# First layer's modulation in two channel chunks on TensorE's column groups, with three projection units interleaved and x loaded first

## The reference

```python
cond_act = silu(cond)                        # c for latent, c_ctx for context tokens
for layer in range(2):
    shift, scale, gate = split(cond_act @ w_mod[layer] + b_mod[layer], 3)
    hm = rmsnorm(x, norm_g[layer]) * (1 + scale) + shift
    if layer == 0:                           # Fourier mixer A | gated conv mixer B
        u_a, z_a, b_b, c_b, v_b, z_b = split(hm @ w_in, 6)          # w_in: 1024 x 6144
        y_a = fft2(u_a in 4 groups of 256 channels, ortho).real * silu(z_a)
        y_b = b_b * dwconv3(c_b * v_b) * silu(z_b)
        out = concat(y_a, y_b) @ w_out
    else:
        out = bidirectional SSD mixer(hm)    # the longer part of the kernel
    x = x + gate * out
return rmsnorm(x, final_norm_g), states
```

## Time and profile before

| | us |
|---|---|
| median of 3 executions | 1209.58 |
| lowest, highest | 1209.22, 1210.56 |
| the profiled execution's own time | 1210.87 |
| its span, first to last instruction | 1208.9 |
| PE busy in it | 1136.6 |
| DVE busy, ACT busy, POOL busy | 792.9, 441.8, 280.5 |

### The profile page before, as it was taken

How to read it: one execution, slowest core, us unless ns; L and a number is a source line. 1 busy time by engine, 2 the same in 40 slices (tenths; PEclk the granted TensorE clock), 3 DMA queues, 4 the chain that set the end, 5 groups by cost and what they waited for, 6 DMA issues and landing times. The chain is left out here.

```text
span 1208.9 us, 19168 instructions
## 1 busy us (share of the span) xinstructions
PE 1136.6 (94%) x7179; PEld 1044.7 (86%) x7179; DVE 792.9 (66%) x1385; ACT 441.8 (37%) x846; POOL 280.5 (23%) x422
## 2 busy tenths in 40 slices
PE   6899999999999999999889999898989898978997
PEld 1389999999999998888889989898989898967786
DVE  1553444467666434547779797979797979786454
ACT  3331222122211133335544544454535453544321
POOL 1110000000000000012043534444443535463001
PEclk9899999999999999999999999999999999989999
DMA  8642223254544243214334333434342424272702
GB/s 332 188 148 68 84 85 104 56 183 128 158 135 143 88 176 102 83 35 158 85 95 123 101 110 105 126 105 127 99 121 87 125 80 144 71 265 63 295 30 87
DMA packets 175670, 148.04 MB, mean 122 GB/s; under 512 B 6844, under 2 KB 156708, under 8 KB 175220
## 3 DMA queue, kind: packets, MB, share of 16 engines
q1 hardware_dynamic: 170996, 130.29, 34.6%
q0 software_dynamic: 4608, 16.83, 4.1%
HBM read 134.31 MB, written 12.78 MB: 122 GB/s over the span
## 5 line engine op out<-in xcount | busy, mean ns | idle before, releaser
L261 DVE TENSOR_TENSOR w_lo<-raw_w,w_hi 128x1024 fp32r<-128x1024 f32 x128 | 157.0, 1230 | 94.6 <-ACT w_hi L255 93.0
L290 PE MATMUL PS<-h_hi,w_hi 128*128 128x320 f32 x768 | 177.2, 312 | 6.1 <-DVE h_lo L364 5.2
L290 PE MATMUL PS<-h_lo,w_hi 128*128 128x320 f32 x768 | 175.6, 310 | 0.0
L290 PE MATMUL PS<-h_hi,w_lo 128*128 128x320 f32 x768 | 175.5, 310 | 0.0
L255 ACT ACTIVATE w_hi<-raw_w 128x1024 fp32r<-128x1024 f32 x128 | 134.2, 1052 | 110.1 <-PE PS L290 72.2
L290 PEld LDWEIGHTS PS<-h_hi,w_hi 128*128 128x128 f32 x768 | 128.4, 189 | 11.2 <-issue 4.0
L290 PEld LDWEIGHTS PS<-h_hi,w_lo 128*128 128x128 f32 x768 | 129.0, 188 | 0.0
L290 PEld LDWEIGHTS PS<-h_lo,w_hi 128*128 128x128 f32 x768 | 128.9, 188 | 0.0
L1320 PE MATMUL PS<-h_hi,w_hi 128*128 128x320 f32 x480 | 118.9, 330 | 10.4 <-DVE big L1509 10.4
L1320 PE MATMUL PS<-h_lo,w_hi 128*128 128x320 f32 x480 | 111.7, 315 | 0.0
L1320 PE MATMUL PS<-h_hi,w_lo 128*128 128x320 f32 x480 | 111.6, 314 | 0.0
(11 more groups left out here) (223 smaller groups left out, 2257.7 us busy)
## 6 DMA issues: line engine op xcount, KB each, us to landing
raw_w<-in_fc_w_in_dram SPq DMA_DIRECT2D x48, 512.0 KB, 4.6
raw_w<-in_ssd_w_in_dram SPq DMA_DIRECT2D x48, 512.0 KB, 5.1
big<-l_scr SPq DMA_DIRECT2D x40, 512.0 KB, 4.1
big<-in_w_mod_dram POOLq DMA_DIRECT2D x16, 1024.0 KB, 5.4
raw_w<-in_fc_w_out_dram SPq DMA_DIRECT2D x16, 512.0 KB, 3.6
raw_w<-in_ssd_w_out_dram SPq DMA_DIRECT2D x16, 512.0 KB, 7.8
big<-in_w_mod_dram SPq DMA_DIRECT2D x6, 1024.0 KB, 18.0
y_scr<-big SPq DMA_DIRECT2D x40, 128.0 KB, 1.8
```

Source lines behind the costliest of these rows:

```text
L261: dve.tensor_tensor(w_lo[:, slot, :], raw_w[:, slot, :], w_hi[:, slot, :].bitcast(F32), ALU.subtract).then_inc(lo_ready, 1)
L290: mm = pe.matmul(PS[:, 2 * pair + s, 0:HALF], w[:, slot, ws], h[:, kt, s * HALF:(s + 1) * HALF], start=(kt == 0 and n == 0), stop=(kt == K ...
```

## The change

- SP loads x first, as five DMAs of one token tile each, then the parameters. The constants and the conditioning vectors are issued on ACT's queue.
- `w_mod`'s shift and scale columns are treated in two chunks: chunk c has channels 512c to 512c+511 of both. A chunk is eight DMAs, one for each set of 128 rows, of 512 KB (2 KB pieces). There is one buffer, so chunk 1 is issued when PE has used chunk 0; units 0 to 2 are loaded between them.
- `cond` is padded with zeros to 32 columns (`condp`). The eight row sets are multiplied in four column groups: row set 4·half+q goes to PSUM partitions 32q to 32q+31. The sum over the groups is made by the product that also turns the row into a column, with a (128, 2) constant `group_sum` as moving operand.
- Shift and scale of channel tiles 0 to 3 are finished from chunk 0, and their `h` made, before chunk 1.
- Units 0, 1 and 2 are summed side by side in three pairs of banks, each in two parts: channel tiles 0 to 3 and 4 to 7.
- ACT does the norm before the SiLU of `cond`.

```diff
-        wm = [carve(5120, 2, 1024), raw_w[:, 0:2, :], raw_w[:, 2:4, :], *(carve(5120 + 2048 * n, 2, 1024) for n in (1, 2, 3)),
-              carve(23808, 2, 1024), carve(5120, 2, 1024)]
+        wm = carve(5120, KT, 2, 512)
+        condp = carve(21504, KT, 32)
...
+        def mod_pe(pe, c):
+            for half in range(2):
+                pe.wait_ge(wm_landed[2 * c + half], 64)
+                for s in range(2):
+                    for q in range(4):
+                        t = 4 * half + q
+                        mm = pe.matmul(PS[32 * q:32 * q + 32, 6 + s, :], condp[:, t, :], wm[:, t, s, :],
+                                       start=(half == 0), stop=(half == 1))
+            mm.then_inc(wm_used, 1)
+        def mod_T_pe(pe, c):
+            pe.wait_ge(mod_copied, c + 1)
+            for j in range(8):
+                mm = pe.matmul(PS[:, 6, 2 * j:2 * j + 2], mod_sb[:, j // 4, (j % 4) * P:(j % 4 + 1) * P], group_sum,
+                               start=True, stop=True)
+            mm.then_inc(mod_T, 1)
...
         def start_pe(pe):
+            for t in range(3):
+                norm_pe_tile(pe, t)
             pe.wait_ge(par_landed, 16 * PAR_DMAS)
             pe.transpose(PS[:, 6, 0:P], praw[:, 0, :], ident)
...
+            for t in range(3, NT):
+                norm_pe_tile(pe, t)
+            pe.wait_ge(cond_padded, 1)
+            pe.wait_ge(par_ready, 2)
+            mod_pe(pe, 0)
+            mod_T_pe(pe, 0)
+            unit_part_pe(pe, 0, range(0, 4))
+            pe.wait_ge(ss_step, 1)
+            mod_pe(pe, 1)
+            unit_part_pe(pe, 1, range(0, 2))
+            mod_T_pe(pe, 1)
+            unit_part_pe(pe, 1, range(2, 4))
+            for u, kts in ((2, range(0, 4)), (0, range(4, 8)), (1, range(4, 8)), (2, range(4, 8))):
+                unit_part_pe(pe, u, kts)
...
+            chunk_load(0)
+            first_load(0)
+            first_load(1)
+            first_load(2)
+            sp.wait_ge(wm_used, 1)
+            chunk_load(1)
+            first_load(3)
+            sp.wait_ge(wm_used, 2)
             sp.dma_start(dft_g, A["dft_group"]).then_inc(dft_landed, 16)
...
+            norm_act(act)
             act.wait_ge(cond_landed, 32)
             act.activation(cond[:, :, :], cond[:, :, :], ACT.Silu).then_inc(cond_ready, 1)
-            norm_act(act, 0, xn, xT0)
-            for u in range(2):
-                split_hi(act, u, u)
-            act.wait_ge(wm_used, 8)
-            act.activation(mod_sb[0:2, 0:1024], PSf[0:2, 0:1024], ACT.Copy).then_inc(mod_copied, 1)
...
+            split_hi(act, 0, 0)
+            mod_copy_act(act, 0)
+            split_hi(act, 1, 1)
+            for k in range(4):
+                h_act(act, k)
+            split_hi(act, 2, 2)
+            mod_copy_act(act, 1)
+            for k in range(4, KT):
+                h_act(act, k)
+            split_hi(act, 3, 3)
...
+            split_lo(dve, 0, 0)
+            dve.wait_ge(par_ready, 2)
+            ss_dve(dve, 0)
+            split_lo(dve, 1, 1)
+            h_dve(dve, 0)
+            split_lo(dve, 2, 2)
+            ss_dve(dve, 1)
+            h_dve(dve, 1)
+            split_lo(dve, 3, 3)
```

More of the change, by code:

```diff
@@ L361, in h_dve @@
+        def h_dve(dve, c):
+            dve.wait_ge(ss_ready, c + 1)
+            if c == 0:
+                dve.wait_ge(xt_done, NT)
+            for k in range(4 * c, 4 * c + 4):
+                for seg, (a, b) in enumerate(SEGS):
+                    dve.tensor_scalar(xT0[:, k, a:b], xT0[:, k, a:b], ss_mod[:, 1, seg, k:k + 1], ss_mod[:, 0, seg, k:k + 1],
                                       ALU.mult, ALU.add).then_inc(v_done, 1)
                 if k % 2:
-                    dve.wait_ge(hh_done, KT * layer + k)
@@ L373, in h_act @@
[L373 to L376 removed]
+                pool.wait_ge(hh_done, k + 1)
+                pool.tensor_tensor(h_lo[:, k, :], xT0[:, k, :], h_hi[:, k, :].bitcast(F32), ALU.subtract).then_inc(h_odd_ready, 1)
+        def h_act(act, k):
+            act.wait_ge(v_done, 2 * (k + 1))
+            act.activation(h_hi[:, k, :], xT0[:, k, :], ACT.Copy).then_inc(hh_done, 1)
@@ L708, in build_step, with mod_copy_act, unit_part_pe @@
         eh_done, el_done = sem("eh_done"), sem("el_done")
+        def mod_pe(pe, c):
+            for half in range(2):
+                pe.wait_ge(wm_landed[2 * c + half], 64)
+                for s in range(2):
+                    for q in range(4):
[9 more added lines that the diff above has]
+            mm.then_inc(mod_T, 1)
+        def mod_copy_act(act, c):
+            act.wait_ge(wm_used, c + 1)
+            act.activation(mod_sb, PS[:, 6:8, :], ACT.Copy).then_inc(mod_copied, 1)
+        def unit_part_pe(pe, u, kts):
+            if kts[0] == 0:
+                pe.wait_ge(lo_ready, u + 1)
+            for kt in kts:
+                if u == 0:
+                    h_wait(pe, 0, kt)
+                ws = slice(kt * P, (kt + 1) * P)
+                for n, (w, h) in enumerate(((w_hi, h_hi), (w_hi, h_lo), (w_lo, h_hi))):
+                    for s in range(2):
+                        mm = pe.matmul(PS[:, 2 * u + s, 0:HALF], w[:, u, ws], h[:, kt, s * HALF:(s + 1) * HALF],
+                                       start=(kt == 0 and n == 0), stop=(kt == KT - 1 and n == 2))
+            if kts[-1] == KT - 1:
+                mm.then_inc(unit_used, 1)
         def start_pe(pe):
+            pe.wait_ge(cst_landed, 16)
+            for t in range(3):
+                norm_pe_tile(pe, t)
             pe.wait_ge(par_landed, 16 * PAR_DMAS)
@@ L768, in fourier_act @@
                 act.wait_ge(unit_used, 4 * i + k + 1)
-                src = pair_view(k % 2)
+                src = pair_view(2 if first and k == 2 else k % 2)
                 if k < 2:
@@ L1855, in _ @@
             dve.memset(ones[:, :], 1.0).then_inc(ones_ready, 1)
+            for t in range(4):
+                norm_dve_tile(dve, 0, xn, t)
             dve.wait_ge(par_T, 1)
@@ L1905, in _ @@
             norm_pool(pool, 0)
-            h_pool(pool, 0, xT0)
+            h_pool(pool)
             mod_pool(pool)
```

174 lines of the change are left out of this document (59 added, 115 removed).

## The result

| | before | after |
|---|---|---|
| median of 4 executions each, us | 1209.4 | 1193.6 |
| lowest, highest | 1209.09, 1210.56 | 1192.75, 1194.93 |
| profiled execution, its span | 1210.87, 1208.9 | 1192.75, 1190.7 |
| first DFT product starts | 85.35 | 69.19 |

The ratio after to before is 0.9869, 95% interval [0.9852, 0.9886]: 15.8 us faster. I had expected 1193.6 within 1 us and a first block of the modulation of 5.3 to 6.1 us; that block took 5.01, so both were missed on the fast side.

What follows compares the result with a forecast made beforehand. The kernel was taken as a PE stream whose start alone could shrink: first DFT product from 85.35 to 70.7, 14.6 us earlier, so 1210.87 becomes 1196.3, less 1.3 for the median gives 1195.0 us; range 1190 to 1202.

Steps and rivals of the forecast that it cites:

- What bounds the kernel: Whole kernel: a PE stream; the first DFT product's start shifts 14.6 us, and the end with it.
- Loads: Start: x lands by 10.2 us, chunk 0 by 21.4, three units' weights by 26.7; chunk 1 by 40.8.
- Norm: ACT's chain and token transposes at 2.2 us each: last copy ends at 19.9, modulation may start at 21.8.
- Column groups: Modulation: a set costs 1.03 us, a chunk 4.1 instead of 13.8; slow start 1.9; chunk 0 used up at 27.8.
- h of 0 to 3, half unit: After chunk 0: h starts at 31.9, tile 3 enters PE 7.6 us later at 39.5, PE free at 40.4.
- From chunk 1 to the DFT: From 44.6: 28 channel tiles take 24.6 us, group sum 1.1, small waits 0.4; DFT starts at 70.7.
- Later loads: Later modulation weights, issued at 57.5, margin 9 us; rival that late slices give the gain back: 1209, chance 0.04.
- slower pieces: Rival on chunk loads: 2 KB pieces at 294 GB/s, 14.3 us a chunk; 1197.8, or 1201.6 with a bubble; chance 0.12.
- latencies paid one by one: Rival on chunk loads: eight loads don't overlap, 28.8 us a chunk, DFT at 104, 1228 us; chance 0.01.
- groups that don't overlap: Rival on modulation: each matmul costs 0.86 us, a chunk 13.8; DFT at 90.0, 1214.2 us; chance 0.05.
- Quicker start: Rival on the start: full PE clock early, modulation at 20.8, chunk 0 done at 25.0; 17.5 us earlier, 1192; chance 0.18.
- Sum: Whole kernel: DFT 14.6 us earlier, profiled execution 1196.3; 1.3 less for the median, 1195.0; chance 0.60.

Runs made afterwards that it cites:

- e3: Changed kernel with unit 0's tiles 0 to 3 done after chunk 1, nothing of unit 0 between the chunks: 1197.94 us, ratio 0.9901.
- e5: Kernel before with only the modulation products spread over four column groups and their sum, loads and order as before: 1210.98 us, ratio 1.0016.
- e1: Changed kernel with all eight row sets summed in one column group instead of four: 1214.66 us, ratio 1.0051.
- v2: v1 with chunk 1 in memory of its own, loaded without waiting for chunk 0, its first half multiplied between unit 0's tiles 1 and 2: 1189.36 us.
- e2: Changed kernel with unit 0 finished first after chunk 1, then units 1 and 2 whole, none side by side: 1200.28 us, ratio 0.9925.
- e4: Changed kernel with x loaded behind chunk 0, and SiLU and chunk 0's products ahead of the norm: 1199.42 us, ratio 0.9918.
- v3: v2 with one table load at the start, SiLU behind the third square, unit 1's weights issued behind chunk 1 and split later: 1191.8 us.
- v4: v2 with 22 filler transposes on PE between chunk 0's group sum and unit 0's first part: 1190.06 us, ratio 0.9843.
- e6: e5 with ACT's and DVE's copies of the modulation moved ahead of their weight splits: 1205.51 us, ratio 0.9967.
- v1: Changed kernel with SiLU and padding before the norm, chunk 0's copy before unit 0's split_hi, unit 1's split_lo behind h 0 to 3: 1192.51 us.

## Why the prediction was right

**What bounds the kernel**: right. The milestone moved by 16.2 us (85.35 to 69.19) where I had 14.6. Behind it the span is 1121.5 us long, before it was 1123.6 (1208.9 - 85.35). Nothing was done there, and in the other ten profiled executions of these kernels and the second of the changed one that stretch was 1119.4 to 1123.3. So it varies by up to 4 us between executions, and 2 of the 18 us that the profiled pair shows lie in that stretch, where nothing was changed. I had taken it as fixed, and had said that I would be wrong if it grew; it did not.

**Loads**: right in what mattered. The last token tile was used at 13.0, chunk 0 never held PE, and 2 KB pieces move at 388 GB/s (I took 401). Chunk 1 was undersized: in e3 it took 14.7 us from issue to the use of its second half, I had 13.0. In the changed kernel, issued at 25.34, that puts its landing near 40.0 (an estimate), and PE wants the second half at about 40.5. It cost nothing only because chunk 0 was used up 2.5 us ahead of my forecast; that is luck.
The Trainium skill (DMA: Bandwidth & Descriptors, Rules for kernel authors) wants at least 1 MiB per DMA for full bandwidth; eight DMAs of 512 KB in flight here moved 385 to 405 GB/s, those of 1 MB in the kernel before 410 to 420. Their pieces differ too (2 and 4 KB), so the runs don't tell which of the two makes the difference.

**Norm**: a term too large. I doubled every tile's transposes to 2.2 us; three tiles took 5.29 us together and the last two 1.09 each. The last copy ended at 18.1, not 19.9, and the table load and SiLU behind it took 1.5 as forecast. The modulation began at 19.94 instead of 21.8.

**Column groups**: right, slightly better: 0.91 us a set (3.64 / 4) for 1.03. The slow start is real, 1.7 us for 1.9 (1.4 and 2.5 in other executions of the same code). The second chunk had none, as forecast, but the clock was back only just before it: 0.71 in the window from 36 to 38, 1.00 from 38. The change of form costs the 0.1 us that I had: the pair of line 737 before the block starts at 38.27, 0.39 ahead of it, where pairs stand 0.29 apart.

**Group sum**: undersized, 1.95 and 1.84 us for 1.1. I had priced eight products by the transposes of a token tile, 0.14 us a piece; a piece is 0.24 here. E5 shows what a piece costs at half clock, 0.44.

**h of 0 to 3, half unit**: 29.96 to 37.59 is 7.6 us, as forecast. **From chunk 1 to the DFT**: 26.9 us for 26.1, and the difference is the group sum; tile 7 came 0.17 late, forecast 0.2.

**Later loads**: the first slice of the other modulation weights was issued at 56.0 and used at 65.2 without a wait. The rivals of slower pieces, latencies paid one by one, and groups that don't overlap are out by the rows above; e1 shows what the last of these would have cost: 6.1 us at the DFT, for which I had 4.7, and 5.3 in the time. In the sum for slower pieces a landing is off by its own terms (30.5 + 14.3 is 44.8, not 45.4), and in "Quicker start" the second half, landed at 21.4, would not have held a product that wants it at 22.9; neither moves the range. "Quicker start" came half true: the modulation started at 19.94, earlier than its 20.8, but at half clock, so that chunk 0 ended at 25.3 (25.0 there), and h started 1.9 us ahead of my forecast.

**Sum**: for the profiled execution 1196.3 was forecast and 1192.75 measured. Of the 3.6 us, 1.5 are the start (norm 1.9, chunk 0 0.7 and chunk 1 0.6 less, the two sums 1.6 more) and 2.1 the stretch behind the DFT. For the median I then took off another 1.3, because the profiled execution of the kernel before lay above its median. Here it lay 0.85 below it. So the forecast of 1195.0 is nearer to 1193.6 than its terms are: two misses of opposite sign partly cancel.

**The stretch behind the DFT**: its length goes with TensorE's granted clock. Behind the DFT the clock falls to 0.50 for some microseconds again and again, and not equally often in every execution. Here is the same work, 550.65 to 552.65 us behind the DFT, in the kernel before and in v2 (windows):

```profile
636.00:638.00 2.00, 2.00 (x10) 2.00 (x10) 1.96 (x8) 0.60 (x1) 1.22 (x2) 0.50 0.97 282
```

```profile
618.32:620.32 2.00, 2.00 (x16) 2.00 (x15) 1.96 (x8) 0.60 (x1) 0.80 (x2) 1.00 0.96 283
```

I add up one minus the clock over windows of 1 us in which it was under 0.97, from the DFT to 1112 us behind it. That gives 8.5 us in v2, 10.2 in e3 and e5, 11.9 to 12.0 in seven profiles (both of the changed kernel, e1, e2, e4, v3, v4) and 13.6 to 13.7 in the kernel before, e6 and v1. In the same order the stretch is 1119.4 us long, 1121.0, 1120.5 to 1122.5, and 1122.6 to 1123.6. So most of the 2.1 us between the profiled pair, and of v2's short rest, goes with such falls of the clock.

**Open**: why the clock falls in one execution and not in another at the same work, and so whether v2 is really 3 us better than the changed kernel. Its DFT is only 1.1 to 1.5 us earlier than in the two profiles of the changed kernel; v3 and v4 with earlier DFTs than v2 had longer medians. Of v2's lead I call only that 1.1 to 1.5 shown.

## What to carry to other kernels

Here thin products (two rows of result) ran 3.8 times as fast in four column groups, but time won on one engine reaches the end only if the next engine's queue is free for it. In e5 the 7.9 us won were more than lost again: 6.9 to two copies that stood behind splits of weights not yet landed (3.8 of waiting, 3.1 of half clock behind it), and 2.7 to the sum over the groups. Look for what stands ahead of the critical copy in each in-order queue, and put work without a deadline (half a unit, a second and third unit side by side) where PE would wait for a landing or for h. Price a wait of PE at its length and at the half clock behind it, and don't read a shift of under 2 us at a milestone from total times of this kernel.

## What the runs showed of the hardware that I had not expected

- A small load is late when large ones share the DMA engines. The load of the context's conditioning vector, 4 KB in 32-byte pieces, landed 1.9 us after its issue in the kernel before, where it was issued ahead of the large loads. Issued at 1.65 to 1.67 on ACT's queue beside x's loads it took 5.6 (v1) to 6.9 us (v2) and held SiLU until 7.31 and 8.60. In e4 it went out on the same queue at the same time, but the first load of 512 KB was issued only at 3.47, and it took 2.9. So it is the large loads and not the queue that holds it. The Trainium skill (DMA: Bandwidth & Descriptors, Issuing engines are not separate DMA queues) says that DMAs issued by several engines run on the same 16 DMA engines and interleave; these rows agree, and here that costs the load 3 to 5 us.
- The same first block of the modulation took 5.34 and 5.01 us in two executions of one kernel and 6.12 in e2 and e3, all after the same 2.93 us of idleness; without that hole it took 3.64 (v2).
- The clock may fall while PE is at work: in v4 it was 0.82 in the window from 26 to 28 and 0.50 in the next, and PE was busy in both without a break, with transposes. At the same point behind the DFT, with PE busy for the whole 2 us, it was 0.50 in one execution (10 matmuls) and 1.00 in another (16).
